# Block hand-over: who splits the weights, and when the sums of the first attention norm are taken

## The reference, cut to what matters

```python
out = jnp.einsum('bsd,de->bse', m, w_out[l])
x = x + gate[:, None, :] * out            # residual of the first block
x = _rmsnorm(x, final_g)
# second block, layer 0: 16 meta tokens in front, 528 rows
h = jnp.concatenate([meta_tokens, x], axis=1)
hn = rms_norm(h, ln_attn_g[0])
q, k, v, qi, ki, wi = jnp.split(hn @ w_in_a, A_SPLITS, axis=-1)
# qi, ki, wi score the keys; top_k picks 128 of them per query; then attention
```

## Time and profile before

| what | value |
|---|---|
| time, median of 3 runs | 2199.8 us (2196.9 to 2200.43) |
| profiled execution, its own time | 2195.71 us |
| its span, first to last instruction | 2194.4 us |
| mean granted TensorE clock | 0.992 |
| PE busy | 2125.9 us (97%) |
| DVE busy | 1463.6 us (67%) |
| ACT busy | 994.8 us (45%) |
| POOL busy | 133.1 us (6%) |

### The profile page before, as it was taken

How to read it: one execution, slowest core, us unless ns; L and a number is a source line. 1 busy time by engine, 2 the same in 40 slices (tenths; PEclk the granted TensorE clock), 3 DMA queues, 4 the chain that set the end, 5 groups by cost and what they waited for, 6 DMA issues and landing times.

```text
span 2194.4 us, 45350 instructions
## 1 busy us (share of the span) xinstructions
PE 2125.9 (97%) x19810; PEld 1869.3 (85%) x19810; DVE 1463.6 (67%) x2479; ACT 994.8 (45%) x1735; POOL 133.1 (6%) x124
## 2 busy tenths in 40 slices
PE   8999999999999989879999999999999999999999
PEld 3877788888778878768889999999988899999987
DVE  5889888887796855965577676334666657766622
ACT  4225655655625343335454444323666654443311
POOL 0000000000000004233410000000000030000000
PEclk9999999999999999999999999999999999999999
DMA  7631011111332533100133223224210023222322
GB/s 292 129 112 50 22 70 46 46 46 46 126 105 87 166 123 108 42 11 20 35 118 96 85 89 95 87 84 141 69 39 30 22 85 107 87 94 90 89 99 72
DMA packets 60021, 184.26 MB, mean 84 GB/s; under 512 B 7184, under 2 KB 11280, under 8 KB 59824
## 3 DMA queue, kind: packets, MB, share of 16 engines
q1 hardware_dynamic: 59824, 181.37, 26.1%
HBM read 174.73 MB, written 6.62 MB: 83 GB/s over the span
## 4 chain that ended last, share of the span: by engine, by line
PE 84%; DVE 9%; ACT 3%; issue 1%; DMA 1%; POOL 0%; SPq 0%; DVEq 0%
PE PS L603 67%; PE PS L788 3%; PE PS L777 2%; DVE ca L2062 2%; PE PS L1148 2%; PE PS L1279 2%; PE PS L797 1%; PE PS L1247 1%; DVE wlo L1960 1%; ACT Lb L1327 1%; DVE Swk L2496 1%; DVE mx L2492 1%; PE PS L1121 1%; PE PS L768 1%; DMA early<-in_wall 1%
## 5 line engine op out<-in xcount | busy, mean ns | idle before, releaser
L603 PE MATMUL PS<-nhi,whi 128*128 128x264 f32 (+1 forms) x2064 | 431.3, 290 | 2.4 <-ACT Vk L1327 1.5
L603 PE MATMUL PS<-nhi,wlo 128*128 128x264 f32 (+1 forms) x2064 | 418.1, 284 | 1.5 <-DVE wlo L1960 1.5
L603 PE MATMUL PS<-nlo,whi 128*128 128x264 f32 (+1 forms) x2064 | 418.6, 284 | 0.0
L1327 ACT ACTIVATE whi<-raw 128x1024 fp32r<-128x1024 f32 (+3 forms) x322 | 306.6, 953 | 199.5 <-PE PS L603 199.5
L1960 DVE TENSOR_TENSOR wlo<-raw,whi 128x1024 fp32r<-128x1024 f32 (+1 forms) x257 | 307.8, 1205 | 88.9 <-ACT whi L1327 88.8
L603 PEld LDWEIGHTS PS<-nhi,whi 128*128 128x128 f32 x2064 | 321.4, 190 | 9.7 <-ACT Vk L1327 1.7
L603 PEld LDWEIGHTS PS<-nhi,wlo 128*128 128x128 f32 x2064 | 320.8, 189 | 1.8 <-DVE wlo L1960 1.7
L603 PEld LDWEIGHTS PS<-nlo,whi 128*128 128x128 f32 x2064 | 321.3, 189 | 0.0
L603 PE MATMUL PS<-hhi,whi 128*128 128x512 f32 x648 | 266.2, 411 | 0.6 <-DVE hlo L2015 0.4
L603 PE MATMUL PS<-hhi,wlo 128*128 128x512 f32 x648 | 256.6, 396 | 7.0 <-DVE wlo L1960 6.9
L603 PE MATMUL PS<-hlo,whi 128*128 128x512 f32 x648 | 254.9, 393 | 0.0
(11 more groups left out here) (390 smaller groups left out, 3479.8 us busy)
## 6 DMA issues: line engine op xcount, KB each, us to landing
raw<-in_wall SPq DMA_DIRECT2D x266, 512.0 KB, 3.6
early<-in_wall SPq DMA_DIRECT2D x16, 512.0 KB, 14.7
raw<-in_wall SPq DMA_DIRECT2D x16, 384.0 KB, 3.1
TZ<-g_rows SPq DMA_DIRECT2D x2, 2112.0 KB, 9.0
raw<-in_wall SPq DMA_DIRECT2D x32, 128.0 KB, 2.0
raw<-in_wall SPq DMA_DIRECT2D x16, 256.0 KB, 2.6
g_rows<-gsb SPq DMA_DIRECT2D x8, 328.0 KB
xt<-in_xT SPq DMA_DIRECT2D x2, 1024.0 KB, 8.5
```

Source lines behind the costliest of these rows:

```text
L603: q = e.matmul(out, cuts[a][:, k * P:(k + 1) * P], (hi_, lo_)[b][:, kr, lo:lo + w], start=start and k == 0 and a == b == 0, stop=stop and ...
L1327: return e.activation(out, src, func, **kw)
```

## The change

Four edits:

1. On DVE, `ahead(i + 3)` of the first `out` unit stands ahead of `mod_end` and of the wait for the residual, instead of behind the first residual add. It covers `out` units 1 and 2.
2. On DVE, `ahead(i + 3)` of the last `out` unit stands behind both remaining `rest` calls.
3. Three `a_in` units (ki, and the first two qi units) are split by DVE instead of POOL; the others stay with POOL.
4. On PE, `first_stats` comes after all 8 blocks of ki instead of after 6, and in the qi units `later` is run one block later (after 7 blocks instead of 6).

```diff
--- before.py
+++ after.py
@@ -30,6 +30,7 @@
          (3, 0), (3, 1), (3, 2), (3, 3)]
 BY_DVE = 1
 ON_POOL = ("a_in", "a_out", "b_out")
+HANDED_OVER = (("a_in", 2048), ("a_in", 1536), ("a_in", 1664))
 
 
 BEFORE = "fftttpftfftptffffpfftftfffttfpffpffffftf"
@@ -505,12 +506,12 @@
         NU = len(units)
         offs, slot, LO = [], [], []
         n = s = 0
-        for what, _, _, nk in units:
+        for what, base, _, nk in units:
             offs.append(n)
             n += P * nk * P
             slot.append(s % NSPL)
             s += what != "ada"
-            LO.append("lo_pool" if what in ON_POOL else "lo_dve")
+            LO.append("lo_pool" if what in ON_POOL and (what, base) not in HANDED_OVER else "lo_dve")
         cut = [i for i in range(NU) if units[i][0] != "ada"]
         before3 = {i: cut[n - NSPL] if n >= NSPL else None for n, i in enumerate(cut)}
         ada_unit = {unit[1:3]: i for i, unit in enumerate(units) if unit[0] == "ada"}
@@ -1042,7 +1043,8 @@
 
             def made_a():
                 b = banks["ki"] = pair_of_banks(("wtok",))
-                yield from steps_of("a_in", b, nhi, nlo, lambda k: on.wait_ge(*at("n0", k)))
+                yield from steps_of("a_in", b, nhi, nlo, lambda k: on.wait_ge(*at("n0", k)), flush_at=8)
+                flush()
 
                 def turn_wi(b=b):
                     on.wait_ge(*at("wi"))
@@ -1054,7 +1056,7 @@
                 yield
                 for k in range(4):
                     b = pair_of_banks(("qi", k))
-                    yield from steps_of("a_in", b, nhi, nlo)
+                    yield from steps_of("a_in", b, nhi, nlo, flush_at=6)
                     yield
                 for name, n in (("ka", 2), ("va", 2), ("qa", 8)):
                     for k in range(n):
@@ -2337,6 +2339,7 @@
             for j in range(8):
                 i = count.take()
                 if j == 0:
+                    ahead(i + 3)
                     mod_end(4)
                     mod_end(5)
                     on.wait_ge(s_res, 16)
@@ -2344,10 +2347,12 @@
                 on.wait_ge(*at("unit", i))
                 e.scalar_tensor_tensor(x2[:, j, :], PS[:, j % 4, :], mod[:, 16 + j:17 + j], x2[:, j, :], ALU.mult,
                                        ALU.add).then_inc(*up("x2", j))
-                ahead(i + 3)
+                if j < 7:
+                    ahead(i + 3)
                 if j:
                     rest(j - 1)
             rest(7)
+            ahead(i + 3)
 
 
             later = []
```

## The result

The changed kernel takes 2189.4 us (median of 4 runs, 2186.2 to 2190.3); the kernel before, run beside it, 2200.1 (2196.9 to 2204.6). The ratio is 0.995, with a 95% interval of 0.9933 to 0.9968. The forecast was 2192.6 us. The profiled execution of the changed kernel took 2186.2 us with a span of 2184.9 and a mean clock of 0.991. One execution of the kernel before (2326.4 us, at a clock of 0.845) was in a slower state than all the others and is left out of every comparison here.

A forecast was written before the change was run, and what follows sets the result against it. PE, busy 97% of the span, was taken as the bound, so only its idle or slow time could be won. 9.45 + 2.6 - 4.8 = 7.2 us less: 2199.8 - 7.2 = 2192.6 us, range 2186.5 to 2198.

The forecast's parts named there:

- Part 1: First `out` units: two splits run on DVE ahead of the residual wait; 9.45 us gained, 6.5 of it idle time.
- The rival of a late residual: At `out` unit 3: two new weight loads delay the residual up to 4.7 us; 2198.6 us in all, chance 0.05.
- the margin: `out` unit 3: DVE's split ends at 783.5, PE needs it at 784.1; it fits by 0.6 us.
- Part 2: First attention unit: three splits leave POOL for DVE; squares ready at t + 5.0, not t + 7.2 (t: last residual add).
- Part 3: First attention units: sums after all 8 blocks need no wait, `turn_wi` gets a new 0.5 us wait; 2.6 us gained.
- Part 4: POOL's queue behind the `TZ` DMA: the third qi unit's split comes late; PE wait and slow clock lose 4.8 us.
- its cover: Third qi unit: without the `ISA` row, POOL's split is done 2.4 to 4.0 us before PE reaches it.
- The 6.8 us for the `ISA` row: POOL, between the `TZ` corner and `H_scaled`: the row priced like the small DMA `keep`, 6.8 us.
- no gap there: Sign on POOL between the `TZ` corner and first `H_scaled`: 6 to 7 us gap expected; without one, the forecast is wrong.
- The rival with the hidden row: POOL's `ISA` row is hidden (under 2.4 us or during the `TZ` wait): 12.05 us gained, 2187.8 us, chance 0.2.
- Behind 866 us nothing else changes: After 866 us all streams start earlier by the same amount, with no other change.
- The lock-out that the prediction put beside PE's path: POOL's remaining splits meeting the selection's adds on DVE: each blocks the other for one split, 2.42 us, beside PE's path.

The follow-up runs named there:

- the run with the residual later: Changed kernel with one 512 KB weight load issued ahead of the residual: median 2189.8 us, ratio 0.9961 to the kernel before.
- the second and third profile: The changed kernel run again, unmodified, two more times: median 2187.4 us (6 runs) and 2187.2 us (1 run).

## Why the prediction was right, and where not

- Part 1 held to 0.1 us. PE reaches ki 45.76 us after the start of `out`, 55.20 before: 9.44, forecast 9.45. The rival of a late residual is out: with the two weight loads behind it, it took 9.7, 10.1 and 10.2 us to land in the three profiles, against 9.4 and 9.3 before, not 4.7 us more. But the margin was about 0.3 us and not 0.6 (the run with the residual later), and in the second and third profile it was used up.
- Part 2 held. Last residual add 811.22, last sum ready 816.70: t + 5.5, forecast t + 5.0. PE needed it at t + 5.6. So the sums are half a microsecond later than worked out, with 0.2 us to spare: the term taken as 2.45 us from the trace before came out at 2.9, because DVE waits there for ACT (0.64 us for `nhi` and 0.28 for `sq_f`).
- Part 3 held. Sums at 816.86 without a wait, `turn_wi` 9.19 later (forecast 9.14), with the new wait of 0.42 that the prediction had at 0.5.
- Part 4 is the step that failed, by the size of one term. Its timing was right: the `TZ` DMA is issued at 818.28 and the corner blanked at 827.45 (t + 16.2, within t + 15.0 to 16.6). So was its cover (PE reaches the split at t + 23.6, forecast t + 23.3; the second qi unit started at t + 16.0, where Part 4 used 15.9 and Part 3's sum gives 16.1). The 6.8 us for the `ISA` row were taken from a small DMA, because the trace had no duration for it; it is 0, and by the prediction's own sign ("no gap there") the forecast is wrong at this part. With that term went the 3.5 us wait and the 1.3 of slow clock. The rival with the hidden row (12.05 us gained, chance 0.2) is the one that happened: 12.1.
- "Behind 866 us nothing else changes" was wrong. The attention stretch is 3.0 us longer in the first profile, beside 13.7 us more at half clock. That loss happened to be near the 4.8 us that part 4 took off by mistake. In the profiled executions the forecast's gain was 7.2 and the measured one 9.5: the sum came out near by luck, through two errors of opposite sign.
- The lock-out that the prediction put beside PE's path can reach it. In the second profile of the changed kernel, DVE's first selection step began during a split of GpSimd (827.60 to 829.97) and ended only behind the three instructions that followed it without a pause. GpSimd, then DVE, then PE:

```profile
829.93 1.29 POOL L2838 TENSOR_TENSOR H<-H,rstd_f 128x512 f32<-128x512 f32 x1
831.19 2.38 POOL L2814 TENSOR_TENSOR wlo<-raw,whi 128x1024 fp32r<-128x1024 f32 x1
833.54 1.27 POOL L2838 TENSOR_TENSOR H<-H,rstd_f 128x512 f32<-128x512 f32 x1
```

```profile
829.38 5.72 DVE L2474 TENSOR_SCALAR Ssc<-rel,wtok 128x528 f32<-128x528 f32 x1 [3.22 <-ACT rel L1329]
```

```profile
836.66 1.17 PE L1100 MATMUL PS<-kiT,qiT 64*128 64x132 f32 x16 [1.92 <-DVE qiT L2378]
```

The same instruction takes 1.84 us in the first profile and 0.73 in the kernel before. PE waited 1.92 us for the step queued behind it, most of the 2.3 by which this hand-over is longer. The prediction's price for a meeting, one split of 2.42 us, can be too small: here it was 5.0 us. It is not always that large: in the first profile GpSimd runs the same row of instructions without a pause, and DVE's step ended after the first of them that followed. What lets DVE in at one of them and not at another no run shows.

## What to carry to other kernels

An instruction whose inputs are ready must not stand behind another's long wait on the same engine: moving two splits ahead of a DMA wait brought 8 of the 12 us, though it left PE only 0.3 us of room. Before an unseen row in a queue is priced, ask whether the engine changes its kind of operation there; here the row was free where it didn't, and where it did, the price could be paid early, while the engine was idle. Time won before a stage with waits is not all kept: read the clock of the stages behind the change too.

## What the runs showed of the hardware

- GpSimd, first use of another kind of operation: gaps of 6.74 us (to partition_broadcast at the start), 7.21 (back to tensor_tensor, 820 us later) and 11.05 (back at once). Without a change of kind 0.05 us, with the same `ISA` row at the place.
- A DVE tensor_scalar (one tensor and one column of scalars from SBUF) took 5.72 us instead of 0.73 while GpSimd ran three instructions beside it without a pause, and 1.84 us in another execution of the same kernel.
- A 2 MB DMA with a 512 KB one issued 0.4 us ahead of it took 9.6 us to land (run with the residual later), against 9.7 without.
- Over whole executions the kernel before had a mean clock of 0.990 (54 executions, 0.985 to 0.994) and the changed one 0.992 (11, 0.991 to 0.995). At 0.991 they took 2197.1 us (mean of 14) and 2189.5 (of 4): 7.6 us apart, where the medians are 10.7 apart. So about 3 us of the gain come with a higher mean clock. The profiles explain this only in part: the stretch of 10.2 us at half clock at PE's 6.46 us wait is gone, but attention has more, and over the whole span the first pair of profiles has 34.7 us at half clock before and 38.7 after.
